# A transformer layer on eight cores: shared temporaries, more exp buffers, and another order of loads and of the first feed-forward round

## What is computed

```python
mod_x = split(silu(c) @ w_ada + b_ada, 6)            # shift, scale, gate, twice
hc = modulate(layer_norm(ctx), mod_c[0], mod_c[1])   # 256 context tokens
kc, vc = context_kv(hc, w_in)
h = modulate(layer_norm(x), mod_x[0], mod_x[1])
q, k, v, u, vb, ga, gb = split(h @ w_in)             # 8 q heads, 2 kv heads of 64
ya = window_attention(rope(q), rope(k), v, kc, vc, sink)   # +-128 tokens, and context
yb = gelu(u) * (w_spatial @ layer_norm(gelu(vb)) + b)      # chunks of 128 tokens
merged = sigmoid(ga) * (ya @ w_a) + sigmoid(gb) * (yb @ w_b)
x_mid = layer_norm(ALPHA * x + mod_x[2] * (merged @ w_o)) * ln1_g + ln1_b
h2 = modulate(layer_norm(x_mid), mod_x[3], mod_x[4])
gate, up = split(h2 @ w_ffn_in)                      # hidden width 2816
x_new = layer_norm(ALPHA * x_mid + mod_x[5] * ((silu(gate) * up) @ w_ffn_out)) * ln2_g + ln2_b
```

## Time and profile before

| | us |
|---|---|
| median of 3 runs (slowest core) | 993.98 (993.93 to 994.42) |
| profiled execution | 995.9 |
| its span on the slowest core (5) | 994.2 |
| spans of the eight cores | 986.5 to 994.2 |
| TensorE busy (matmul) | 903.3 (91%) |
| VectorE, ScalarE, GpSimd busy | 625.7, 321.9, 274.7 |
| first matmul of the feed-forward | 507.94 |
| end of the last matmul | 976.9 |

### The profile page before, as it was taken

One profiled execution on the slowest core, in us unless ns is written; L12 is line 12 of the kernel. 1 busy time (PEld: TensorE's weight loads), 2 busy tenths in 40 slices (PEclk: granted clock), 3 DMA queues, 4 the chain that ended last, 5 costly groups with the idle time before them and its releaser, 6 DMA issues.

```text
span 994.2 us, 15838 instructions; the slowest of 8 cores (986.5 to 994.2 us)
## 1 busy us (share of the span) xinstructions
PE 903.3 (91%) x5589; PEld 446.8 (45%) x5589; DVE 625.7 (63%) x1130; ACT 321.9 (32%) x497; POOL 274.7 (28%) x234
## 2 busy tenths in 40 slices
PE   1389879887999999999979999999999999999993
PEld 0335534444445444444434444444444444444761
DVE  4437877836555348886686565556655574666677
ACT  0426775547776114443334201111011101110111
POOL 6023353636434233333320630202202021000004
PEclk9999978977999999999999999999999999999997
DMA  8998912378300950027412451303213020111112
GB/s 196 196 191 195 224 50 86 70 124 121 59 2 3 249 111 1 2 85 127 105 23 95 132 149 49 85 0 85 32 54 85 0 43 1 43 48 59 44 64 85
DMA packets 30236, 83.91 MB, mean 84 GB/s; under 512 B 2896, under 2 KB 3152, under 8 KB 28496
## 3 DMA queue, kind: packets, MB, share of 16 engines
q0 software_dynamic: 18064, 34.54, 22.1%
q1 hardware_dynamic: 12096, 48.37, 14.1%
HBM read 109.05 MB, written 8.39 MB: 118 GB/s over the span
## 4 chain that ended last, share of the span: by engine, by line
PE 81%; DMA 7%; DVE 5%; issue 3%; POOL 2%; ACT 2%; DVEq 0%; POOLq 0%; SPq 0%; ACTq 0%
PE psum L1168 30%; PE psum L1193 15%; PE psum L1006 11%; PE psum L1057 5%; PE psum L1023 5%; DMA arena<-wqk 4%; PE psum L663 3%; PE psum L719 3%; PE psum L890 2%; PE psum L926 2%; DMA arena<-xh 2%; DVE arena L493 2%; PE psum L750 1%; DMA arena<-wada 1%; ACT arena L896 1%
## 5 line engine op out<-in xcount | busy, mean ns | idle before, releaser
L1168 PE MATMUL psum<-arena 128*128 128x512 bf16 (+1 forms) x1536 | 318.7, 363 | 5.5 <-ACT arena L1174 5.5
L1168 PEld LDWEIGHTS psum<-arena 128*128 128x128 bf16 x1536 | 150.7, 98 | 161.7 <-issue 9.3
L1174 ACT ACTIVATE arena<-psum 128x512 f32<-128x512 f32 (+1 forms) x96 | 53.8, 562 | 373.3 <-PE psum L1168 373.2
L1193 PE MATMUL psum<-arena 128*128 128x512 bf16 x704 | 163.2, 379 | 0.0
L1207 DVE TENSOR_TENSOR arena<-arena,psum 128x512 f32<-128x512 f32 x224 | 140.6, 681 | 30.2 <-PE psum L1193 30.1
L1176 DVE TENSOR_TENSOR arena<-psum,arena 128x512 bf16<-128x512 f32 (+1 forms) x96 | 61.9, 646 | 133.3 <-PE psum L1168 130.2
L500 POOL TENSOR_TENSOR arena<-arena 128x1 f32<-128x1 f32 (+1 forms) x74 | 47.9, 648 | 288.7 <-DVE arena L498 282.7
L1006 PE MATMUL psum<-arena 128*128 128x512 bf16 x512 | 118.0, 379 | 0.0
L493 DVE BATCH_NORM_STATS2 arena<-arena 128x6 f32<-128x512 f32 x152 | 98.2, 683 | 15.4 <-ACT arena L760 7.1
L1193 PEld LDWEIGHTS psum<-arena 128*128 128x128 bf16 x704 | 68.6, 98 | 82.3 <-issue 1.7
L896 ACT ACTIVATE arena<-psum 128x1024 bf16<-128x1024 f32 (+1 forms) x100 | 81.1, 851 | 18.6 <-PE psum L890 16.0
(11 more groups left out here) (97 smaller groups left out, 902.6 us busy)
## 6 DMA issues: line engine op xcount, KB each, us to landing
arena<-xh SPq DMA_DIRECT2D x34, 512.0 KB, 9.7
arena<-wada POOLq DMA_DIRECT2D x24, 512.0 KB, 13.9
arena<-wff POOLq DMA_DIRECT2D x11, 1024.0 KB, 10.1
arena<-wff SPq DMA_DIRECT2D x11, 1024.0 KB, 7.0
out<-arena SPq DMA_DIRECT2D x16, 512.0 KB, 2.6
arena<-wc POOLq DMA_DIRECT2D x8, 768.0 KB, 11.9
arena<-wout SPq DMA_DIRECT2D x8, 512.0 KB, 4.2
arena<-rope SPq DMA_DIRECT2D x4, 512.0 KB, 15.4
```

Of the source, the lines that this page charges most:

```text
L1168: ins = e.matmul(bank(ps)[:, 0:n], lhsT=w1v[r][:, k, lo:lo + 128], rhs=h2(k), start=(k == 0), stop=(k == 7))
L1174: s = P.op('act', prio - 150, act_cost(n), lambda e: e.activation(out=sgv(), in_=bank(pg)[:, 0:n], func=AF.Silu), after=[a], takes=[sg], g ...
L1193: ins = e.matmul(bank(ps), lhsT=actv[(r, fi, t)], rhs=w2v[r][:, fi, h * 512:(h + 1) * 512], start=(n == 0), stop=(n == 2 * len(rounds) - 1))
```

## The change

It has five parts.

1. `gv` and `sg` are one pool (`sg`). The first merges (group 0) use three of its buffers. A gate block may be queued once the v matmuls are (`wvvb_done`), no longer behind `gv_done` and `raw_done`.
2. Tiles 0 to 3 have nine `pt` buffers: five as before, four where the halo lay (`U0`). So their exps come after `hal_done`, and wc1_0 and wc1_1, which are loaded to the same place, come after the first eight products with v (tiles 0 to 3).
3. Group 2 is normalized ahead of `hal`: its call has priority 29 and comes first, where it had 50 and came later.
4. Pieces 12 to 23 of ada get priorities of 100 to 113, where they had 160 to 173, and use banks 0 and 1 in place of 4 and 5.
5. Round 0: `act_free` is the eight output blocks of the tiles 8 to 11 for one buffer and 12 to 15 for the other, where both had waited for all 32; and `swap` is 0 for a Silu.

Beside these, the cost numbers of a dozen operations are set closer to what they take, and `norm_group` may normalize on GpSimd (no call does). These numbers only steer the planner.

```diff
@@ norm_group calls
+    norm_group('2', [xh[(9 + i) * 128:(10 + i) * 128, :] for i in range(4)], 29, [ld_wu[3]])
     norm_group('hal', [xh[0:128, :], xh[17 * 128:18 * 128, :], ctxb[0:128, :], ctxb[128:256, :]], 30, [ld_wu[3]])
...
-    norm_group('2', [xh[(9 + i) * 128:(10 + i) * 128, :] for i in range(4)], 50, [ld_wvvb])
     norm_group('3', [xh[(13 + i) * 128:(14 + i) * 128, :] for i in range(4)], 64, [ld_wu[1]])
@@ v
-            gv = slot('gv', 0, 1, 2)
+            gv = slot('sg', 0, 1, 2)
@@ ada
-        ada(12 + c, [(3, c), (4, c)], 160 + c, (0, 1), after=[t_wo[-1]], apart=True)
+        ada(12 + c, [(3, c), (4, c)], 100 + c, (0, 1), after=[t_wo[-1]], psb=(0, 1), apart=True)
...
-        ada(20 + n, [(5, 2 * n), (5, 2 * n + 1)], 170 + n, (0, 1), after=[t_wo[-1]], apart=True)
+        ada(20 + n, [(5, 2 * n), (5, 2 * n + 1)], 110 + n, (0, 1), after=[t_wo[-1]], psb=(0, 1), apart=True)
@@ attend
+    o_pt = [L['pt'] + 2 * KB * i for i in range(5)] + [o_xn, o_xn + 2 * KB] + [U0 + 2 * KB * i for i in range(4)]
...
-                    after=[mm, xn_free if len(pts) > 5 else None], behind=list(ex), takes=[pt] if kv[0] == 0 else [], gives=[sp], tab=EXPSET)
+                    after=[mm, hal_done if j < 4 else xn_free], behind=list(ex), takes=[pt] if kv[0] == 0 else [], gives=[sp], tab=EXPSET)
...
-            attend(j, 62.0 + 4 * j, (6, 7), (4, 5), (0, 1, 2, 3, 4))
+            attend(j, 62.0 + 4 * j, (6, 7), (4, 5), (0, 1, 2, 3, 4, 7, 8, 9, 10))
@@ merge
-    room = {0: hal_done, 1: hal_done + wqk_done, 2: wqk_done, 3: wu_done, 4: wu_done + wvvb_done, 5: wvvb_done,
+    room = {0: hal_done + pv_last[:8], 1: hal_done + pv_last[:8] + wqk_done, 2: wqk_done, 3: wu_done, 4: wu_done + wvvb_done, 5: wvvb_done,
...
-        slots = (0, 1, 2, 3)
+        slots = (0, 1, 2, 3) if g > 0 else (0, 1, 2)
...
-            mm = P.op('pe', prio, 1.73, f, after=hneed(g) + [ld_wc1[m]], behind=[order, gv_done, raw_done, mg_free[g]], takes=[ps])
+            mm = P.op('pe', prio, 1.73, f, after=hneed(g) + [ld_wc1[m]], behind=[order, wvvb_done, mg_free[g]], takes=[ps])
...
-                      after=[mm, gv_done, raw_done], takes=[sg], gives=[ps], tab=TANHSET)
+                      after=[mm, raw_done if g > 0 else None], takes=[sg], gives=[ps], tab=TANHSET)
@@ feed-forward
-    act_free = [wo_all, wo_all]
+    act_free = [[wo_done[(t, h)] for t in ts for h in range(2)] for ts in (range(8, 12), range(12, 16))]
...
+        s.swap = 0.0
```

More of the change, by code:

```diff
@@ L499, in stat @@
             out=mv[:, sid(st):sid(st) + w, 4], in0=mv[:, sid(st):sid(st) + w, 1], scalar1=eps, scalar2=None, op0=ALU.add), after=b)
-        r = P.op('pool', prio - 40, 0.6, lambda e: e.tensor_tensor(
+        r = P.op('pool', prio - 40, 0.75, lambda e: e.tensor_tensor(
             out=mv[:, sid(st):sid(st) + w, 2], in0=mv[:, sid(st):sid(st) + w, 4], in1=neghalf[:, 0:w], op=ALU.pow),
@@ L537, in norm_pair @@
             order = [xn_last[0]]
-            if engs[i] == 'dve':
-                n = P.op('dve', prio, 0.72, lambda e, i=i, xbv=xbv: e.tensor_scalar(
+            if engs[i] != 'act':
+                n = P.op(engs[i], prio, 0.83 if engs[i] == 'dve' else 1.6, lambda e, i=i, xbv=xbv: e.tensor_scalar(
                     out=xbv(), in0=xvs[i](), scalar1=mean_of(st, i), scalar2=rstd_of(st, i), op0=ALU.subtract, op1=ALU.mult),
@@ L590, in build_nc @@
         ada_ld.append(ada(c, [(0, c), (1, c)], 0.5 + c, range(8), psb=(0, 1, 2, 3)))
-        t_h[(0, c)] = P.op('dve', 1.5 + c, 0.26, lambda e, c=c: modulate_out(
+        t_h[(0, c)] = P.op('dve', 1.5 + c, 0.41, lambda e, c=c: modulate_out(
             e, 'dve', hT[:, c, 0:512], hT[:, c, 0:512], 1, 0, c, 0), after=[raw0[c], modc_ready[(0, c)], modc_ready[(1, c)]])
@@ L617, in put @@
                     eng = 'act' if c2 % 2 == 0 or name != 'hal' else 'dve'
-                    cost = 0.8 if eng == 'act' else 0.45
+                    cost = 0.78 if eng == 'act' else 0.61
                     need = [tr] + [modc_ready[(kd, c)] for kd in (0, 1)]
@@ L763, in proj_v @@
             mi = minus(st, prio + i - 20, r)
-            z = P.op('act', prio + i - 20, 0.62, lambda e, st=st, gvs=gvs: e.activation(
+            z = P.op('act', prio + i - 20, 0.82, lambda e, st=st, gvs=gvs: e.activation(
                 out=gvs(), in_=gvs(), func=AF.Identity, scale=rstd_of(st), bias=minus_of(st)), after=[mi], gives=[st])
@@ L881, in attend @@
             pt_of[n] = pt
-            ptv = lambda pt=pt: V(L['pt'] + 2 * KB * sid(pt) if sid(pt) < 5 else o_xn + 2 * KB * (sid(pt) - 5), BF16, 8, 128)
+            ptv = lambda pt=pt: V(o_pt[sid(pt)], BF16, 8, 128)
             ex = []
@@ L904, in attend @@
                 me = 'dve' if s == 2 and j >= 4 else 'pool'
-                ex = P.op(me, prio + n * 0.1, 1.1 if me == 'dve' else 2.2, lambda e, ptv=ptv, mi=mi: e.tensor_tensor(
+                ex = P.op(me, prio + n * 0.1, 1.0 if me == 'dve' else 2.1, lambda e, ptv=ptv, mi=mi: e.tensor_tensor(
                     out=ptv(), in0=ptv(), in1=masks[:, mi:mi + 1, :].to_broadcast([128, 8, 128]), op=ALU.mult),
@@ L923, in f @@
                         pt = pt_of[n]
-                        pv = V(L['pt'] + 2 * KB * sid(pt) if sid(pt) < 5 else o_xn + 2 * KB * (sid(pt) - 5), BF16, 8, 128)
+                        pv = V(o_pt[sid(pt)], BF16, 8, 128)
                         vs = vaug[:, j + s, kv, 0:65] if kd == 'w' else vcaug[:, s, kv, 0:65]
@@ L1097, in residual @@
                     c = 4 * c4 + ci
-                    t_h2[(g, i // 2, c)] = P.op('act', prio + i, 0.5, lambda e, ps=ps, ci=ci, c=c, cut=cut: modulate_out(
+                    t_h2[(g, i // 2, c)] = P.op('act', prio + i, 0.57, lambda e, ps=ps, ci=ci, c=c, cut=cut: modulate_out(
                         e, 'act', hT[:, c, cut], bankb(ps)[:, ci * 256:(ci + 1) * 256], 4, 3, c, 0),
```

## The result

The changed kernel takes 982.53 us (median of 4 runs, 981.92 to 983.19) against 993.95 for the kernel before beside it: a ratio of 0.9885 (0.9867 to 0.9902), 11.4 us faster. The forecast was 974.5 with 966 to 985 as its range. The direction and the range held, the size was 8 us too large. In some executions the cores of a die are granted a lower clock and the whole takes some per cent longer; all times given here leave such executions out.

The account below looks back on a forecast made before the run. TensorE was taken as the bound from 241.4 us, with gains in one hole near 508 and in idle, slow-clock stretches ahead; -1.5 -0.5 -4.5 -4.5 -0.4 -8.1 = -19.5, and 995.9 - 19.5 - 1.9 = 974.5 us, range 966 to 985.

Parts of the forecast that it names:

- Term 4: Round 0 of the feed-forward: the first Silu comes earlier, its product no longer waits for all of wo_done; 8.1 us gained.
- The turns of tiles 14 and 15: In round 0, next possible late item: needed at 542.9 us, their chain ready at 540.9, so fitting by 2.0.
- Term 3: Tile 4 to feed-forward: earlier merges fill TensorE between S blocks, 4.5 us gained; moving the ada pieces, 0.4 more.
- rival C: Attention from tile 4 on: wada loads gate the merges, so the kernel is slower by 5.7, 1000 us; chance 0.05.
- The clock that I wanted over 0.9 from 200 to 240: Sign of Term 3 at tile 4: TensorE's granted clock over 0.9 from 200 to 240 us.
- Term 1: 95.1 to 132.2 us, group 2 ahead of halo and context: new wait, but group 3's waits fall; 1.5 us gained.
- some 7: Part of Term 1: of the 12.1 us from 98.89 to 111, TensorE is idle for some 7, where 2.9 stood.
- Term 2: Tiles 0 to 3, nine exp buffers: 0.5 us gained in tiles 0 and 1, 4.5 in tiles 2 and 3.
- the sentence under the sum: Whole kernel: the changed cost numbers are the planner's and change only the order; no time was counted for them.
- The sign of term 2: In the profile after, no TensorE wait over 1 us for exps in tile 3.
- The start of the feed-forward: Test of terms 1 to 3: they are wrong if it still starts within 4 us of 507.9.
- rival A: Halo chain costs more than it gives: Term 1 loses 4, Term 2 gains 0.5 and 2; 982.5 us, chance 0.14.

Follow-up runs that it names:

- g4: The kernel before with swap = 0 for Silu alone, act_free left as it was: 0.9915, 985.5 us.
- e4: The changed kernel with all five parts but the cost numbers of the kernel before: 0.9802, 974.3 us.
- f2: The five parts with the old cost numbers, but part 2 undone (five exp buffers): 0.9775, 971.6 us.
- e3: The changed kernel, new cost numbers kept, with part 2 undone (five exp buffers, no wait of wc1_0 and wc1_1): 0.9963, 990.3 us.
- e1: The kernel before with part 5 alone (act_free by halves, swap 0 for Silu): 0.9915, 985.5 us.
- e5: The kernel before with nothing but the new cost numbers: 1.0063, 1000.2 us.
- g2b: f2 with one new cost number, 0.75 for 0.6 for the power on GpSimd: 0.9792, 973.3 us.
- e2: The changed kernel, new cost numbers kept, with part 3 undone (halo and context normalized ahead of group 2): 0.9869, 981.0 us.
- g1: The changed kernel, queues in the same order, with GpSimd's two masks of tile 2 cut to 8 of 128 columns: 978.96 and 981.03 us.

## Why the prediction was right and where it was not

**Term 4, round 0: right.** Forecast 8.1; the loss there went from 7.8 to 0.0, and part 5 alone gained 8.4 in time. The mechanism (Silu behind eight L570) is shown by g4. What was wrong is a half sentence: the product's wait for all of `wo_done` didn't matter. The turns of tiles 14 and 15 fitted, as worked out. The first Silu runs 0.02 us behind its table load in the changed kernel too, so no drain is seen there.

```profile
505.02 1.28 ACT L1175 ACT_TABLE_LOAD   x1 [1.33 <-PE psum L1169]
506.32 0.60 ACT L1175 ACTIVATE arena<-psum 128x512 f32<-128x512 f32 x1
```

**Term 3, merge and ada: right in size.** Forecast 4.9 together; the loss from tile 4 to the feed-forward fell by 4.7 (12.7 to 8.0), and undoing parts 1 and 4 in e4 raised it from 8.2 to 13.3. From 90 us on the changed kernel waits for no wada load; rival C found nothing to stand on. Whether part 1 or part 4 brought it was not tried. The clock that I wanted over 0.9 from 200 to 240 came to 0.89.

**Term 1, group 2 first: the place and the sum of the waits right, what holds them wrong.** There are 6.7 us of waits between 98 and 107 for "some 7", and none of 4 near 129. But I had TensorE wait for the turns of halo and context until their normalizations end near 111. They end at 108.73 (L543 of 106.36, 2.37 long), and the turns at 112.22 wait 0.43. The 6.7 come ahead of them. The 3.01 at 100.86 are ahead of turns of group 2 itself (ScalarE writes them out as 128x512, those of halo and context as 128x256): the L476 that frees their bank stands in VectorE's queue behind statistics of the context, which had waited 2.75 for the load. The 2.56 at 106.27 ended when VectorE was past L797, which had waited 1.32 for a load, and the small instructions behind it. So the late halo and context cost time through VectorE's queue, and that the sum agrees is luck. In e4 it is the same: 2.80 at 102.09, with 2.23 for a context load on VectorE. In the changed kernel the loss ahead of tile 0 rose by 0.5, which is within the noise of the losses; with the old numbers it fell by 2.4, where I had 1.5.

**Term 2, nine exp buffers: wrong.** For tiles 0 and 1 I had a gain of 0.5; they lose 4.6 more. For tiles 2 and 3 I had 4.5; they gained 1.5. Two steps failed. The first is the sentence under the sum that the changed cost numbers "change only the order": I took that as a reason for counting nothing. The order is what the parts change in these stretches too, and that of the new numbers cost 8.3 us (e4). The bounds of my terms had no entry for it. The second is the reason given for the term itself. With the old numbers tiles 2 and 3 lose 6.9 where before lost 12.6, a gain of 5.7, so the size looks right; but f2, with five buffers, loses 7.3 there. The buffers are not what brings it. In the changed kernel, with the new numbers, undoing part 2 does cost 7.8 us in all (e3), but not in the place that I named: tiles 2 and 3 lose only 0.6 more. The sign of term 2 came true without the buffers as well: the longest wait for an exp in tiles 2 and 3 was 2.0 to 2.5 us on every core of before, e1 and g4, and at most 0.66 in f2, e3, e5 and g2b, which have five buffers too, and 0.84 in the rest. Which part brings the gain with the old numbers stays open: without part 3 it is 8.6, without parts 1 and 4 it is 6.9, with part 5 alone 12.4, so any two of the three groups seem enough, and single ones weren't run.

**The start of the feed-forward.** I called terms 1 to 3 wrong if it still came within 4 us of 507.9. On the slowest cores it went from 507.94 to 503.05, but in the median of the cores from 502.8 to 500.1, so by the fairer reading they were wrong together, as the three columns above say. Reading the sum off the one slowest core of before, which was 5 us behind the median there, was a weakness of its own.

**The rivals.** The time is that of rival A to the microsecond, but not for A's reason: A wanted 4 us lost in term 1 (measured: 0.5) and only 2 gained in tiles 2 and 3 (measured: 1.5). It missed the 4.6 in tiles 0 and 1. Part of that is the 3.07 us at 155.26, where the spatial product waits for a normalized v that GpSimd finishes only behind a rotation sum, which had itself waited 2.16 for VectorE. It stands on all eight cores of the changed kernel (2.6 to 3.1), and on none when part 3 is undone (e2, 8.9) or the numbers are (e4, 9.9). Of the 9.9 us of loss that e4 has less (8.3 in time), some 4 (tiles 2 and 3 lose 11.1 with them, 6.9 without, 6.6 in g1) are contention of VectorE and GpSimd in one place. The rest, 2.9 us ahead of tile 0 and 3.1 in tiles 0 and 1, is other waits in another order, the 3.07 among them, and no run isolates one of them.

## What to carry to other kernels

A number that a list scheduler plans with is a change of the program, even a truer one: one of them moved this kernel by 14.7 us, so such a number has to be timed alone, and a part that looks good or bad beside it (part 2 here) has to be tried with both sets. Before judging an order, look in the timeline for instructions that take several times their usual length; they show engines in each other's way, which no estimate by single durations has. The fastest kernel found is f2, parts 1, 3, 4 and 5 with the old numbers: 0.9775, 971.6 us.

## What the runs showed of the hardware

A VectorE instruction with two SBUF inputs, 0.69 us by itself, took 4.30 beside three GpSimd instructions in a row and 6.95 beside four, and ended about 0.55 us behind the last of them in both cases. That VectorE can stand back through a whole run of GpSimd, and not share with it, I had not expected. It doesn't always: in e4 the product began beside one GpSimd instruction and ended within the next (1.60 us). Of the 1792 spatial products in the fourteen traces 67 took over 3 us, and all of these lie in kernels with at least one new number. What decides between the two was not found. GpSimd was held up less: its masks took 2.12 in the median and 3.11 at most. VectorE's instructions that read PSUM and one SBUF operand were not held: L682 and L688 kept their 0.68 and 0.69 beside the same GpSimd work in g2b, and no such instruction of 512 columns took over 0.69 in any of the traces.
